# Odd attention: logits by three reduced passes, reciprocals turned and spread by one pass of ones

## What is computed

```python
def odd_layer(hn, rel_bias, w_in, w_out, q_g, k_g):
    q, k, v, gate, qi, ki, wi = split_cols(hn @ w_in, ODD_SPLITS)
    q = rms_norm(q.reshape(bsz, L, C_HEADS, C_HEAD_DIM), q_g)      # 8 heads of 128
    k = rms_norm(k.reshape(bsz, L, C_KV_HEADS, C_HEAD_DIM), k_g)   # 2 heads
    ...
    att = dsa_attention(q, k, v, qi, ki, wi, rel_bias)
    return (att * jax.nn.silu(gate)) @ w_out

# in dsa_attention, per block of 128 queries, with the selected keys idx
logits = einsum(q_blk, k_sel) * Dh ** -0.5
logits = where(valid, logits + bias, NEG_INF)
p = softmax(logits)
out = einsum(p, v_sel)
```

## Time and profile before

| | |
|---|---|
| median of 3 runs | 2011.0 us (2010.79 to 2011.02) |
| profiled execution | 2010.99 us |
| its span | 2009.7 us |
| mean granted clock of PE | 0.993 |
| attention of the odd layer | about 811 to 984 us of the span |

### The profile page before, as it was taken

One profiled execution on the slowest core, in us unless ns is written; L12 is line 12 of the kernel. 1 busy time (PEld: TensorE's weight loads), 2 busy tenths in 40 slices (PEclk: granted clock), 3 DMA queues, 4 the chain that ended last, 5 costly groups with the idle time before them and its releaser, 6 DMA issues.

```text
span 2009.7 us, 24201 instructions
## 1 busy us (share of the span) xinstructions
PE 1944.4 (97%) x9108; PEld 1504.4 (75%) x9108; DVE 1438.2 (72%) x2198; ACT 882.5 (44%) x1573; POOL 620.8 (31%) x428
## 2 busy tenths in 40 slices
PE   8999989999999999999999999999999999999997
PEld 6777867787548787666787887888777877777785
DVE  7668686522379997455357799899997887685639
ACT  5343285333457751545212333544226764352431
POOL 3554410552101122545352000000003673235443
PEclk9999999999999999999999999999999999999999
DMA  6322330442501122311333211111142223455322
GB/s 271 128 72 83 114 123 22 167 158 69 151 22 33 53 76 82 105 42 53 123 98 105 74 54 63 53 53 53 57 147 86 79 74 145 163 191 195 112 85 105
DMA packets 72428, 197.90 MB, mean 98 GB/s; under 512 B 11182, under 2 KB 20559, under 8 KB 71800
## 3 DMA queue, kind: packets, MB, share of 16 engines
q1 hardware_dynamic: 72168, 196.35, 28.9%
q10 hardware_dynamic: 144, 0.00, 0.0%
HBM read 152.89 MB, written 46.71 MB: 99 GB/s over the span
## 4 chain that ended last, share of the span: by engine, by line
PE 47%; DVE 30%; ACT 4%; issue 3%; DMA 2%; POOL 1%; SPq 0%; DVEq 0%; ACTq 0%
PE psum L266 44%; DVE m L2973 10%; DVE m L2187 4%; PE psum L269 3%; DVE m L2994 2%; DVE m L321 2%; DMA m<-in_w 1%; POOL m L311 1%; ACT m L301 1%; DVE m L540 1%; DVE m L456 1%; DVE m L531 1%; DVE m L3172 1%; DVE m L3111 1%; DVE m L3175 1%
## 5 line engine op out<-in xcount | busy, mean ns | idle before, releaser
L266 PE MATMUL psum<-m,m 128*128 128x512 f32 (+10 forms) x8308 | 1862.1, 393 | 40.1 <-DVE m L321 9.8
L266 PEld LDWEIGHTS psum<-m,m 128*128 128x128 f32 (+4 forms) x8308 | 1418.6, 186 | 454.0 <-issue 137.7
L311 POOL TENSOR_TENSOR m<-m,m 128x1024 fp32r<-128x1024 f32 (+1 forms) x122 | 307.9, 2527 | 1002.3 <-ACT m L301 1002.2
L301 ACT ACTIVATE m<-m 128x1024 fp32r<-128x1024 f32 (+2 forms) x166 | 173.4, 1048 | 342.1 <-PE psum L266 208.5
L2973 DVE SCALAR_TENSOR_TENSOR m<-m,m,m 128x1024 f32<-128x1024 f32 x240 | 312.3, 1303 | 6.3
L269 PE MATMUL psum<-m,m 128*128 128x128 f32 x784 | 110.6, 277 | 12.1 <-ACT m L1450 6.1
L269 PEld LDWEIGHTS psum<-m,m 128*128 128x128 f32 x784 | 89.6, 141 | 33.3 <-ACT m L1450 8.0
L2187 DVE TENSOR_SCALAR_CACHE_REDUCE m<-m,m 128x896 bf16<-128x896 f32 (+4 forms) x130 | 102.8, 847 | 1.1
L2519 POOL TENSOR_TENSOR m<-m,m 128x384 f32<-128x384 f32 (+5 forms) x48 | 72.5, 1528 | 55.9 <-DVE m L2311 37.2
L2407 ACT ACTIVATE m<-m,m 128x1024 bf16<-128x1024 f32 (+1 forms) x62 | 64.1, 1035 | 26.4 <-DVE m L2214 26.4
L2311 DVE CUSTOM_DVE_ANT_0 m<-psum,m 128x128 f32<-128x128 f32 (+3 forms) x64 | 48.3, 755 | 37.9 <-PE psum L266 36.7
(11 more groups left out here) (314 smaller groups left out, 1652.9 us busy)
## 6 DMA issues: line engine op xcount, KB each, us to landing
m<-in_w SPq DMA_DIRECT2D x164, 512.0 KB, 3.7
scr_hscr<-m SPq DMA_DIRECT2D x4, 2048.0 KB, 6.6
m<-scr_hscr SPq DMA_DIRECT2D x4, 2048.0 KB, 10.6
scr_turned<-scr_strip SPq DMA_DIRECT2D x8, 575.5 KB, 12.6
m<-in_x SPq DMA_DIRECT2D x4, 1024.0 KB, 7.9
scr_gscr<-m SPq DMA_DIRECT2D x16, 256.0 KB, 4.2
m<-in_x SPq DMA_DIRECT2D x2, 2048.0 KB, 8.8
m<-scr_turned SPq DMA_DIRECT2D x8, 512.0 KB, 4.5
```

The source lines that it names most:

```text
L266: return self.nc.tensor.matmul(out, lhsT, rhs, start=start, stop=stop, skip_group_check=True)
L301: k.nc.scalar.activation(k.hi[SLOT[i]][:, 0:kk * n], k.raw[i % 2][:, 0:kk * n], ACT.Copy).then_inc(*k.up("w_hi", i))
L311: k.nc.gpsimd.tensor_tensor(lo, raw, hi.bitcast(F32), ALU.subtract).then_inc(*k.up("w_lo", i))
```

## The change

The logits are computed by `mm3` from high and low parts. The parts of q and k are made in the attention loop or ahead of it: high by ACT (`query_high`, `key_high`), low by POOL in place (`query_low`, `key_low`). The reciprocals are written as high and low columns of a 36-column strip (`O.rp`, high at 0 to 3, low at 32 to 35), which one transpose turns into a ring bank (`recT`, at the end of the iteration of b = 6, or of b = 2 of the next head); DVE spreads it with a mask to 36 x 512 (`O.rd`), and one pass of ones over 36 rows puts the sum of both parts on all partitions, behind the values' products. A head now takes 16 banks of the ring.

```diff
@@ PE
         for c, e in O.chunks(b):
-            ins = k.mm(k.bank(bank + c // 512)[:, 0:e - c], O.QT[:, n, 128 * b:128 * b + 128], O.KT[:, n // 4, c:e], True, True)
+            ins = k.mm3(k.bank(bank + c // 512)[:, 0:e - c], (O.qh[n % 2][:, bs], O.QL[:, n, bs]), (O.kh[kv][:, c:e], O.KL[:, kv, c:e]), True, True)
...
-    def s3(n, Q):
+    def s3a(n, Q):
+        bank = k.bank(O.ptb.take("recT", n, Q))
+        pe.wait_ge(*O.ptb.freed("recT", n, Q))
+        pe.wait_ge(*at("od_rec", n, Q))
+        k.tr(bank[0:36, 0:128], O.rp[Q]).then_inc(*up("od_recT_ps", n, Q))
+
+    def s3b(n, Q):
         bank = k.bank(O.ptb.take("rec", n, Q))
         pe.wait_ge(*O.ptb.freed("rec", n, Q))
-        pe.wait_ge(*at("od_rec", n, Q))
-        for i in range(4):
-            ins = k.mm(bank[:, 128 * i:128 * i + 128], O.recs[Q][:, i:i + 1].to_broadcast([128, 128]), k.ident, True, True)
-        ins.then_inc(*up("od_rec_ps", n, Q))
+        pe.wait_ge(*at("od_rd", n, Q))
+        k.mm(bank, O.one[0:36].to_broadcast([36, 128]), O.rd[n // 4][0:36].rearrange("p i q -> p (i q)"), True, True).then_inc(*up("od_rec_ps", n, Q))
...
             s3(O.units[i - 4][0], O.units[i - 4][1] // 4)
+            s3b(O.units[i - 4][0], O.units[i - 4][1] // 4)
         if 2 <= i <= len(O.units) + 1:
             s2(*O.units[i - 2])
+        if 3 <= i < len(O.units) + 3 and O.units[i - 3][1] % 4 == 3:
+            s3a(O.units[i - 3][0], O.units[i - 3][1] // 4)
@@ DVE
         if u == 18:
             settle()
+            dve.wait_ge(*last("bits"))
+            V.memset(k.tiny[:, 0:72], 0.0).then_inc(*up("od_rclear"))
+            V.tensor_tensor(O.rmask, k.ident[:, 0:4], k.ident[:, 32:36], ALU.add).then_inc(*up("od_rmask", 0))
+            V.tensor_copy(O.one, k.ones[:, 0:1]).then_inc(*up("od_rmask"))
...
     def s1b(n, Q):
...
-        V.reciprocal(O.recs[Q], O.sums[Q]).then_inc(*up("od_rec", n, Q))
+        dve.wait_ge(*at("od_rclear"))
+        high, low = O.rp[Q][:, 0:4], O.rp[Q][:, 32:36]
+        V.reciprocal(O.recs[Q], O.sums[Q]).then_inc(*up("od_rec", n, Q, "whole"))
+        if n:
+            dve.wait_ge(*at("od_recT_ps", n - 1, Q))
+        dve.wait_ge(*last("od_rec"))
+        V.tensor_copy(high.bitcast(F32R), O.recs[Q]).then_inc(*up("od_rec", n, Q, "high"))
+        dve.wait_ge(*last("od_rec"))
+        V.tensor_tensor(low, O.recs[Q], high, ALU.subtract).then_inc(*up("od_rec", n, Q))
+
+    def s3a(n, Q):
+        bank = k.bank(O.ptb[("recT", n, Q)])[0:36, 0:128]
+        dve.wait_ge(*at("od_recT_ps", n, Q))
+        dve.wait_ge(*at("od_rmask"))
+        if (n, Q) != (0, 0):
+            dve.wait_ge(*at("od_rec_ps", *before((n, Q), 1, 2)))
+        V.tensor_tensor(O.rd[n // 4][0:36], bc(bank, 1, 4), bc(O.rmask[0:36], 2, 128), ALU.mult).then_inc(
+            *up("od_rd", n, Q, also=[("free", "od_ptb", "recT", n, Q)]))
...
+            s3a(O.units[i - 4][0], O.units[i - 4][1] // 4)
             s3(O.units[i - 4][0], O.units[i - 4][1] // 4)
@@ ACT
+        A.activation(O.kh[kv], O.KT[:, kv, :], ACT.Copy).then_inc(*up("od_kh", kv))
...
+        A.activation(O.qh[n % 2], O.QT[:, n, :], ACT.Copy).then_inc(*up("od_qh", n))
...
+        if m == 3:
+            key_high(0)
+        if m == 5:
+            act.wait_ge(*at("keep", 5))
+            query_high(0)
...
+        if i < len(O.units) and O.units[i][1] == 2 and O.units[i][0] < 7:
+            query_high(O.units[i][0] + 1)
+        if i < len(O.units) and O.units[i] == (1, 4):
+            key_high(1)
@@ POOL
+        G.tensor_tensor(O.KL[:, kv, o], O.KT[:, kv, o], O.kh[kv][:, o].bitcast(F32), ALU.subtract).then_inc(*up("od_kl", kv, half))
...
+        G.tensor_tensor(O.QL[:, n, o], O.QT[:, n, o], O.qh[n % 2][:, o].bitcast(F32), ALU.subtract).then_inc(*up("od_ql", n, half))
...
     for name in panels[:-1]:
         pool_panel(k, PANEL_AT[name] + 4)
+        if name in ("og4", "og5"):
+            key_low(0, int(name == "og5"))
+        if name == "og6":
+            query_low(0, 0)
+            query_low(0, 1)
...
+        if i + 1 < len(O.units) and O.units[i + 1][1] in (5, 6):
+            n, half = O.units[i + 1][0], O.units[i + 1][1] - 5
+            if n < 7:
+                query_low(n + 1, half)
+            if n == 2:
+                key_low(1, half)
```

More of the change, by code:

```diff
@@ L1898, in __init__ @@
         self.MH, self.ML = k.tile(PH, [8, 1024], F32R), k.tile(X0 + 32 * KB, [8, 1024], F32R)
+        self.QL, self.KL = k.tile(PH, [8, 1024], F32R), k.tile(PH + 32 * KB, [2, 1024], F32R)
+        self.qh = [k.tile(O + 4 * KB, [1024], F32R), k.tile(H0 + 16 * KB, [1024], F32R)]
+        self.kh = [k.tile(O, [1024], F32R), k.tile(X0 + 60 * KB, [1024], F32R)]
         self.smr = [k.tiny[:, 128 + 8 * i:136 + 8 * i] for i in range(3)]
+        self.rp = [k.tiny[:, 36 * i:36 * i + 36] for i in range(2)]
+        self.rmask, self.one = k.tiny[:, 72:76], k.tile(k.T0 + 352, [1], F32R)
+        self.rd = [k.tile(o, [4, 128], F32R) for o in (X0 + 56 * KB, O)]
         self.sums, self.recs = ([k.tiny[:, o + 4 * i:o + 4 * i + 4] for i in range(2)] for o in (152, 160))
@@ L2072, in s1 @@
             pe.wait_ge(*at("head", O.norms[-1], 1))
-        pe.wait_ge(*at("head", n, b // 4))
+        kv, bs = n // 4, slice(128 * b, 128 * b + 128)
+        pe.wait_ge(*at("od_qh", n))
+        pe.wait_ge(*at("od_kh", kv))
+        pe.wait_ge(*at("od_ql", n, b // 4))
         for half in range(b // 4 + 1):
-            pe.wait_ge(*at("head", 8 + n // 4, half))
+            pe.wait_ge(*at("od_kl", kv, half))
         bank = O.pairs[b % 2]
         for c, e in O.chunks(b):
-            ins = k.mm(k.bank(bank + c // 512)[:, 0:e - c], O.QT[:, n, 128 * b:128 * b + 128], O.KT[:, n // 4, c:e], True, True)
+            ins = k.mm3(k.bank(bank + c // 512)[:, 0:e - c], (O.qh[n % 2][:, bs], O.QL[:, n, bs]), (O.kh[kv][:, c:e], O.KL[:, kv, c:e]), True, True)
         ins.then_inc(*up("od_S", n, b))
@@ L2090, in s2, with s3 @@
             ins.then_inc(*up("od_PT_ps", n, b, j0, also=[("od_P_turned", n, b)] if j0 + 4 > b else ()))
-    def s3(n, Q):
+    def s3a(n, Q):
[4 more added lines that the diff above has]
+    def s3b(n, Q):
         bank = k.bank(O.ptb.take("rec", n, Q))
         pe.wait_ge(*O.ptb.freed("rec", n, Q))
-        pe.wait_ge(*at("od_rec", n, Q))
-        for i in range(4):
-            ins = k.mm(bank[:, 128 * i:128 * i + 128], O.recs[Q][:, i:i + 1].to_broadcast([128, 128]), k.ident, True, True)
-        ins.then_inc(*up("od_rec_ps", n, Q))
+        pe.wait_ge(*at("od_rd", n, Q))
+        k.mm(bank, O.one[0:36].to_broadcast([36, 128]), O.rd[n // 4][0:36].rearrange("p i q -> p (i q)"), True, True).then_inc(*up("od_rec_ps", n, Q))
+    def s3(n, Q):
         for b in range(4 * Q, 4 * Q + 4):
@@ L2421, in head, with key_high, query_high @@
             *up("head_raw", n, half, also=[("free", "od_proj", *use)]))
+    def key_high(kv):
+        for half in range(2):
+            act.wait_ge(*at("head", 8 + kv, half))
+        if kv:
+            act.wait_ge(*at("og_ps", 7, 1))
+        A.activation(O.kh[kv], O.KT[:, kv, :], ACT.Copy).then_inc(*up("od_kh", kv))
+    def query_high(n):
+        for half in range(2):
+            act.wait_ge(*at("head", n, half))
+        if n == 1:
+            act.wait_ge(*at("og_out", 7))
+        if n >= 2:
+            act.wait_ge(*at("od_S", n - 2, 7))
+        A.activation(O.qh[n % 2], O.QT[:, n, :], ACT.Copy).then_inc(*up("od_qh", n))
     def key_value(what, *key):
@@ L2508, in pool_odd, with key_low, query_low @@
     panels = ["qi0", "qi1", "qi2", "qi3", "ki", "ok0", "ok1", "ov0", "ov1", *(f"oq{m}" for m in range(8)), *(f"og{m}" for m in range(8))]
+    def key_low(kv, half):
+        o = slice(512 * half, 512 * half + 512)
+        pool.wait_ge(*at("od_kh", kv))
+        G.tensor_tensor(O.KL[:, kv, o], O.KT[:, kv, o], O.kh[kv][:, o].bitcast(F32), ALU.subtract).then_inc(*up("od_kl", kv, half))
+    def query_low(n, half):
+        o = slice(512 * half, 512 * half + 512)
+        pool.wait_ge(*at("od_qh", n))
+        G.tensor_tensor(O.QL[:, n, o], O.QT[:, n, o], O.qh[n % 2][:, o].bitcast(F32), ALU.subtract).then_inc(*up("od_ql", n, half))
     for name in panels[:-1]:
         pool_panel(k, PANEL_AT[name] + 4)
+        if name in ("og4", "og5"):
[3 more added lines that the diff above has]
+            query_low(0, 1)
     def s0(n, b):
```

## The result

The changed kernel takes 2034.96 us (median of 4, 2033.86 to 2035.39) against 2011.01 (2010.79 to 2012.63): the ratio is 1.0114, 95% interval 1.0102 to 1.0126. It is 24 us slower, where 27 more were forecast.

What follows compares the result with a forecast made beforehand. PE's matmul stream was taken to bound attention at 21.44 us a head. A shorter stream plus new waits adds 25 us over the heads, and 1.9 comes ahead of attention: 2010.99 + 25 + 1.9, so 2038 us, range 2012 to 2048.

Steps and rivals of the forecast that it cites:

- The contention: In attention, POOL's work blocks DVE's new cast and subtraction behind each reciprocal; they last 1 to 2 us.
- First half: At Q = 0, the transpose of reciprocals waits for the blocked operations and a ring bank: PE waits 2.8 us a head.
- Second half: At Q = 1, serial gate multiplies and a blocked subtraction: PE waits 1.4 us a head, where it waits 0.2 now.
- The stream: PE's matmul stream in attention drops from 21.4 to about 20.3 us a head, at best 19.2.
- Logits: In attention, three fp32r passes replace each fp32 product: 1.1 us less a head, 0.6 less at the 128-column ceiling.
- Reciprocals: Turning them on PE costs 1.8 us a head for 1.78, two 0.28 us round trips per half: gain nothing.
- The sum of a head: Attention's period: 20.3 + 2.8 + 1.4 + 0.1 = 24.6 us, 3.2 more a head; 25 in all.
- worse: Rival in attention: dear 128-column products add 5 us, or a clock fall 13 more (2043 to 2052); chance 0.12.
- Ahead of attention: DVE's chain before attention grows 1.9 us: 0.6 for three small operations, 1.3 for a block by key_low on POOL.
- One block per group: Rival in attention's first half: the cast gets in before POOL, only the subtraction is blocked; 2029 us, chance 0.2.
- No contention: Rival in attention: such small operations are not blocked; query_low ahead of bm(7) and serial multiplies remain; 2018 us, chance 0.12.
- The faster case: Rival in attention: nothing contends, tile changes are free, bm(7) is in time; period 20.1, 2002 us, chance 0.11.

Runs made afterwards that it cites:

- e11: Kernel before with only a cast and a subtraction of 4 elements added behind each reciprocal, results unread: 2019.2 us, ratio 1.0025.
- e1: Changed kernel without cast and subtraction; the reciprocal writes the rounded high part, its low part is left out: 2018.9 us, ratio 1.0026.
- e2: Changed kernel with the cast replaced by a second reciprocal that writes the rounded high part: 2023.9 us, ratio 1.0046.
- e5: Changed kernel with both halves of query_low (and of key_low in head 2) on POOL behind bm(5): 2025.8 us, ratio 1.0063.
- e6: Kernel before with the logits' part alone, both halves of query_low behind bm(5), of key_low(0) behind panel og6: 2005.8 us, ratio 0.9963.
- e8: e7 with the pass of ones ahead of the values' products and DVE's spread ahead of block 7's mask operation: 2025.6 us, ratio 1.0069.
- e7: Changed kernel with query_low and key_low placed as in e6, a second reciprocal for the high part, four ACT activations for the low: 2013.7 us, ratio 1.0009.
- e4: Kernel before with the reciprocals' part of the change alone, logits in fp32, no query_low or key_low: 2026.3 us, ratio 1.0060.
- e10: e7 with the four activations of the low part behind ACT's copy of that iteration, not ahead of it: 2009.3 us, ratio 0.9976.
- e9: Changed kernel with 16 unread transposes ahead of the first half's 36-column transpose in heads 1 to 7: 2028.8 us, ratio 1.0078.

## Why the prediction was right, by its own steps

**The contention.** Right, and shown: by the rows of the change, by its appearance in the kernel before when only the two operations are added (e11), and by its loss when they go (e1), are of another kind (e2), or POOL's operation moves (e5). A cast of four elements, with one SBUF input, is held for what is left of POOL's operation, as is the subtraction with two; the reciprocal never is. The row that the prediction gives for the reciprocal (903.28) doesn't show that, since POOL starts as it ends (903.45); e2's row at 932.77 does. The Trainium skill ("SBUF — State Buffer", Who interferes with whom) says that a cast can contend with GpSimd, in its two-port mode, and that an instruction with two SBUF inputs does, and the rows agree with it: 1.88 for 0.17 and 1.18 for 0.16.

**First half.** Forecast: cast done 2.16 after L(4)'s end, the subtraction 3.6, transpose 5.2, a wait of 2.8. Measured from 917.06: 2.0, 3.2, 4.8, idle 2.13, so 2.3. The term was too high by 0.5: DVE's operation ends with POOL's, where I had added 0.17 behind it, twice; PE came at 2.5, as forecast (2.4).

**Second half.** Forecast 1.4 more than before: 0.8 for the transpose, 0.3 and 0.5 for ring banks, less 0.2 taken for the kernel before, whose rows show no idle time. Measured 0.60 and 0.38, so 1.3 with what the rows leave out: the transpose as forecast, the banks some 0.3 less. The reason that I gave for the banks, the serial multiplies behind the ones product, fits the rows. The 0.38 is released by an ACT copy (L2543). Ahead of that ACT makes the high part of the gated output (904.21), which waits 0.26 for the second multiply, and the exponential of block 0, which waits for DVE's mask operation behind both multiplies. Counted from the start of the six transposes ahead of them, that mask operation comes at 1.76 and the copy at 2.49 in the change (902.66, 904.42, 905.15), and at 1.25 and 2.04 in e6 (909.13, 910.38, 911.17), where only one multiply stands there. In e8, which has the multiplies apart, the mask operation comes at 1.26, and the wait is 0.73 for the 1.13 of e7. No run takes the multiplies apart with ACT's copy free of the activations, so this is argued from rows and not shown by an experiment of its own.

**The stream.** Forecast 20.3, measured 19.8. *Logits:* 1.1 less forecast, 1.2 measured (21.45 to 20.23 in e6). A pass of 128 columns is near the floor that I took (0.11) and far from the ceiling of 0.22: three of them in the changed kernel's timeline below last 0.53 with an end of 0.28, which leaves 0.125 a pass, the first of them behind transposes. *Reciprocals:* forecast 1.8 for 1.78, a gain of nothing; measured a gain of 0.5 (e4 less its waits, 20.9; e10 against e6, 19.7 to 20.2). This term was mis-sized, by the number of round trips, which I took at 0.28 each from 16-row products and two per half, because I held that both new operations use fewer rows of the array:

```profile
921.82 0.29 PE L269 MATMUL psum<-m,m 128*36 128x128 f32 x1 [2.13 <-DVE m L2365]
921.86 0.48 PE L266 MATMUL psum<-m,m 128*128 128x512 f32 x1
...
925.27 0.39 PE L266 MATMUL psum<-m,m 128*128 128x128 f32 x2
...
925.62 0.46 PE L266 MATMUL psum<-m,m 36*128 36x512 f32 x1
...
926.01 0.33 PE L269 MATMUL psum<-m,m 128*128 128x128 f32 x1
...
926.64 0.53 PE L266 MATMUL psum<-m,m 128*128 128x128 f32 x3
```

The 36-column transpose is followed after 0.04: it uses all 128 rows and narrows the columns to 36, and no change of shape is to be seen in its rows. The 36-row product starts 0.13 later than in the stream (0.35 for two products at 0.11) and is followed after 0.39 for 0.227, 0.16 more: 0.3 a round trip, as forecast, but one per half and not two.

**The sum of a head.** 24.6 forecast, 23.37 measured at the full clock: 8 x 1.2, some 10 us too high. The clock, which I had left to a rival (worse) with a chance of 0.12, put some 5 back (4.7 by e9's distances). That the total came closer (2038 against 2035) than its parts did is luck. Attention from its first to its last mask operation is 181.07 against 161.64, 19.4 longer, the last multiply of the gate ends 1.1 later behind the last L(7), since two now follow PE in a row, and 0.9 lie behind attention, in code that the change doesn't touch: 2.3 + 19.4 + 1.1 + 0.9 are the 23.7 between the spans.

**Ahead of attention.** Forecast 1.9, measured 2.3 (first mask operation at 813.30 for 811.02), but not from the parts named. The three small operations cost 0.16 in all and not 0.6, and by 770 us nothing is left of that; key_low's contention costs 0.95 and not 1.3; 1.3 was there at 741 us, ahead of all that the change touches, from stretches with a granted clock of 0.97 (300 to 400) less one that was 0.98 before (600 to 700). DVE itself was 2.9 late until then, and got 1.6 of it back by the same contention: its operation of 2 elements, which POOL's panel held for 2.35 in the kernel before, took 0.80 in the change (741.34), as that panel came only 1.3 later. Such falls of the clock are in other executions too, the kernel before's included. The change's own share is 0.95: half of the forecast, and the total was met by luck.

**The rivals.** One block per group (2029) is refuted: in the heads 1 to 6 both were blocked in the first half, with the cast 0.04 to 0.05 behind POOL's start; which of the two comes first was a near thing. No contention is refuted. Its remainder, query_low ahead of bm(7), is real: 1.05 in e1, as I had worked out (1.1), hidden in the change behind the longer wait. The faster case (2002, period 20.1) did not come: even where nothing of the change contends (e10), the period is 20.29 and the time 2009.3, 0.24% below before. The fastest kernel, e6 at 2005.8, is the logits' part alone.

**Open.** Why the clock falls behind three of the six waits of 2.13 to 2.17 us and not behind the others: that such waits cost through the clock is supported by e9, but not when they do. And the whole of the 0.38 wait for ACT's copy: a wait there is in each kernel with 16 banks a head and in none with 14, and only by rows is it put down to the serial multiplies.

## What to carry to other kernels

Before adding a cast, a copy or a two-input operation from SBUF to SBUF on DVE, look in the trace for what POOL does at that moment: its size doesn't matter, POOL's does, and what stands behind it on DVE pays. A cheap substitute for it is a one-input operation that isn't blocked (here a second reciprocal, 0.2 us), or POOL's own work moved to where nobody small waits. Split a change into its parts before judging it: here one part alone is 0.4% faster than before once POOL's operations are placed, and the other part costs 0.6% by itself (e4).

## What of the hardware was not expected

- A reciprocal with a rounded output takes 0.15 to 0.18 us under POOL's work (e2, e7), where a cast of the same four elements takes 1.88.
- DVE's blocked operation ends with POOL's own end, to 0.03 us, with its work in that time.
- A product that narrows the columns (128 x 36) is followed after 0.04 us and shows no cost beside full ones; one that narrows the rows (36 x 512) costs 0.3 us a round trip.
- With idle times of 1.82 and of 2.13 to 2.17 us on PE the granted clock fell in four of the change's stretches of 25 us, to 0.91 at the lowest, where the waits of 1.2 us in e5 left it at 1.00 from 825 on. With sixteen useless products in the wait of 2.13 it stayed at 1.00, and attention was 4.7 us shorter (one profiled execution of each).
